# Hybrid recurrent decoder step: sample parts with input buffers and state loads of their own, filler matmuls one contraction step at a time between their state products, and the next mixer's first chunk prepared inside the first of them

## The reference

```
proj = rmsnorm(x) @ w_in                       # 1024 -> 12 x 512 mixer columns, 16 row values, 3 x 1024 gates
A: mLSTM, B: gated DeltaNet, C: HGRN2          # each with a state (heads=4, 128, 128) per sequence
x += w_out( sum_b sigmoid(gate_b) * w_branch_b(mixer_b) )
x += w_down( relu(w_up rmsnorm(x))^2 )
```

```
o_t = S_t^T q_t          S_new = decay * S + sum_s k_s v_s^T      # for each of 8 sequences and 4 heads
```

## Time and profile before

| | |
|---|---|
| time, median of 3 runs | 2506.95 us (2506.61 to 2510.07) |
| the profiled execution | 2505.12 us, of which the span from first to last instruction is 2503.3 us |
| PE busy | 2322.1 us, 93% of the span |
| DVE, ACT, POOL busy | 939.6, 836.6, 635.9 us |
| share of PE in the chain that ended last | 74% |
| mean granted TensorE clock | 0.956 |

### The profile page before, as it was taken

The page is one execution under the profiler, slowest core; times in us unless marked ns, Lnnn a source line. Parts: engine busy times, 40 slices in busy tenths (PEclk is TensorE's granted clock), DMA queues, the critical chain, the costliest instruction groups (busy, mean ns, idle before and its releaser), DMA issues.

```text
span 2503.3 us, 38224 instructions
## 1 busy us (share of the span) xinstructions
PE 2322.1 (93%) x14767; PEld 2255.5 (90%) x14767; DVE 939.6 (38%) x1388; ACT 836.6 (33%) x1477; POOL 635.9 (25%) x433
## 2 busy tenths in 40 slices
PE   4999699999888999999999989996999999999997
PEld 4999699999868999987999979896999999999996
DVE  5756333333135546414444245625212112212214
ACT  4366222322105555422333123323332332332232
POOL 1222223324025445321111132220222222222121
PEclk9999899999868999988999889998999999999998
DMA  4212424222212232235444255420111011111112
GB/s 156 70 60 95 131 80 115 92 80 85 85 55 91 85 110 80 77 99 157 135 135 135 84 168 183 144 100 34 35 47 58 29 50 54 38 42 54 46 34 86
DMA packets 172547, 218.78 MB, mean 87 GB/s; under 512 B 22156, under 2 KB 126476, under 8 KB 172348
## 3 DMA queue, kind: packets, MB, share of 16 engines
q1 hardware_dynamic: 149388, 178.19, 23.9%
q10 hardware_dynamic: 23088, 39.59, 4.2%
HBM read 160.09 MB, written 57.66 MB: 87 GB/s over the span
## 4 chain that ended last, share of the span: by engine, by line
PE 74%; DVE 10%; issue 7%; DMA 4%; ACT 3%; POOL 2%; SPq 1%; DVEq 0%; ACTq 0%; POOLq 0%
PE D L333 59%; PE M L1471 2%; DVE g_dq L773 2%; PE M L1478 2%; PE M L1481 1%; PE M L678 1%; POOL w_lo L314 1%; DVE m_rd L1614 1%; DVE xn_lo L1788 1%; PE M L1700 1%; PE M L1430 0%; ACT g_sg L708 0%; PE M L1497 0%; DMA g_in<-proj 0%; DVE g_Ss L942 0%
## 5 line engine op out<-in xcount | busy, mean ns | idle before, releaser
L333 PE MATMUL D<-xn_hi,w_hi 128*128 128x352 f32 x2808 | 944.2, 336 | 60.9 <-ACT stage L352 29.7
L333 PE MATMUL D<-xn_hi,w_lo 128*128 128x352 f32 x2808 | 911.6, 325 | 0.0
L333 PE MATMUL D<-xn_lo,w_hi 128*128 128x352 f32 x2808 | 911.4, 325 | 0.0
L333 PEld LDWEIGHTS D<-xn_hi,w_hi 128*128 128x128 f32 x2808 | 536.9, 191 | 78.5 <-ACT stage L352 34.8
L333 PEld LDWEIGHTS D<-xn_lo,w_hi 128*128 128x128 f32 x2808 | 538.1, 192 | 4.7 <-issue 3.8
L333 PEld LDWEIGHTS D<-xn_hi,w_lo 128*128 128x128 f32 x2808 | 535.5, 191 | 0.0
L314 POOL TENSOR_TENSOR w_lo<-w_raw,w_hi 128x1024 fp32r<-128x1024 f32 (+1 forms) x105 | 244.2, 2326 | 729.5 <-ACT w_hi L308 729.4
L333 PE MATMUL D<-y_hi,w_hi 128*128 128x352 f32 x960 | 311.1, 324 | 15.0 <-DVE y_lo L1851 11.1
L314 POOL TENSOR_TENSOR w_lo<-e,w_hi 128x512 fp32r<-128x512 f32 (+1 forms) x96 | 164.3, 1712 | 608.1 <-ACT w_hi L308 608.1
L333 PE MATMUL D<-y_lo,w_hi 128*128 128x352 f32 x960 | 311.4, 324 | 0.0
L333 PE MATMUL D<-y_hi,w_lo 128*128 128x352 f32 x960 | 310.8, 324 | 0.0
(11 more groups left out here) (353 smaller groups left out, 2655.0 us busy)
## 6 DMA issues: line engine op xcount, KB each, us to landing
w_raw<-in_w_proj SPq DMA_DIRECT2D x73, 512.0 KB, 3.6
proj<-stage ACTq DMA_DIRECT2D x61, 528.0 KB, 2.7
e<-in_w_full SPq DMA_DIRECT2D x32, 512.0 KB, 3.5
e<-in_w_half SPq DMA_DIRECT2D x64, 256.0 KB, 2.6
stage<-proj SPq DMA_DIRECT2D x24, 528.0 KB, 3.5
d_bc<-rowd SPq DMA_DIRECT2D x32, 256.0 KB, 6.0
m_in<-proj SPq DMA_DIRECT2D x32, 256.0 KB, 3.8
proj<-u_o SPq DMA_DIRECT2D x12, 528.0 KB, 2.9
```

The source lines that it names most:

```text
L333: last = nc.tensor.matmul(D[b][:, 0:GN], w[t.slot][:, k, :], x[:, k, cols], start=(k == 0 and n == 0), stop=(k == kt - 1 and n == 2))
```

## The change

1. **Buffers of their own.** The sample parts read from `sx_*` (gdn), `gx_h` (hgrn), `mx_h` and `mx_bc` (mlstm). SP loads them, and the 2 MB of states, in the middle of the mixer's loop, between chunks 3 and 4; the loop of SP is cut in two for it. The arenas are laid out anew so that the states (all at the same offset) no longer share memory with what the chunks use.
2. **The last chunk prepares the sample part,** in the places where other chunks prepare the next chunk.
3. **Fillers in one-k pieces.** In the sample parts a group of dense work is cut in 8 pieces (3 matmuls each), and a slot stands after each head of state products and after each head's `kv` (`su`) product. `sample_states` is split into decay, spread, add and kv for one head at a time, and these are placed from the first head's output on.
4. **The first HGRN2 chunk** is prepared inside gdn's sample part: its loads are issued at the start of it, and `hgrn_first` (called as `between(0..2)`) and `hgrn_rest` place the six parts. `clear_hg` moves behind the last two adds.
5. SP issues each mixer's first chunk, the prompt state's store and the remaining weight tiles in a new order, and the DMA scratch size is given as 1024.

```diff
-        def sample_states(kind, eng, steps_of, kv, read, S, decay, vt, vx, kt, banks):
+        def sample_states(op, eng, h, steps_of, kv, read, S, decay, vt, vx, kt, banks):
+            if op == "decay":
+                eng.wait_ge(*pe_.after(f"{read}{h}"))
...
+            if op == "spread":
+                if h >= 2:
+                    eng.wait_ge(*pe_.after(f"{kv}{h - 2}"))
...
+            if op == "kv":
+                eng.wait_ge(*dve_.after(f"vx{h}"))
+                if h >= 2:
+                    eng.wait_ge(*dve_.after(f"s2{h - 2}b"))
...
-        def whole_hgrn_prep(kind, eng, sample, slot):
+        def hgrn_first(kind, eng, at):
+            for part in {"dve": [(0,), (1, 2, 3), ()], "act": [(0,), (1,), (2,)], "pool": [(0,)]}[kind][at]:
+                hgrn_prep(kind, eng, 0, 0, part, False)
+            if kind == "dve" and at == 2:
+                clear_hg(eng)
+
+        def hgrn_rest(kind, eng, slot):
+            for some in {"dve": [(4,), (5,), (), ()], "act": [(3,), (4,), (5,), ()], "pool": [(1,), (), (), ()], "pe": [(), (), (), ()]}[kind]:
                 for part in some:
-                    hgrn_prep(kind, eng, 0, 0, part, sample)
-                if at < 4 and not sample:
-                    slot()
+                    hgrn_prep(kind, eng, 0, 0, part, False)
+                slot()
...
+                    if part == 4 and not follows:
+                        eng.wait_ge(ready, 3)
                     for j in range(L)[:4] if part == 4 else range(L)[4:]:
...
+                if sample:
+                    between(0)
+                    eng.wait_ge(*act_.after("vn"))
+                    states("spread", 0)
+                    states("spread", 1)
+                    states("add", 0)
+                    states("spread", 2)
+                    states("add", 1)
+                    states("spread", 3)
+                else:
...
                 if sample:
-                    sample_states(*states)
-                slot()
+                    between(1)
+                    states("add", 2)
+                    states("add", 3)
+                    between(2)
...
                         for b in range(DEC_BATCH):
                             c = h * N + b * DEC_SEQ
-                            i = eng.matmul(M[0][:, c:c + DEC_SEQ], d_Ss[:, b, h, :], d_pb[:, c:c + DEC_SEQ], start=True, stop=True)
-                    i.then_inc(*pe_.step("ks"))
+                            i = eng.matmul(M[0][:, c:c + DEC_SEQ], d_Ss[:, b, h, :], B.pb[:, c:c + DEC_SEQ], start=True, stop=True)
+                        if h == H - 1:
+                            i.then_inc(*pe_.step("ks"))
+                        slot()
...
-        mixers = (("gd", gdn, LOOP_GD, GD_SLOTS, GD_SLOTS, [3, 2, 2, 2, 2, 4] + [3, 3, 3, 3], 3),
-                  ("hg", hgrn, LOOP_HG, HG_SLOTS, HG_SLOTS, [9, 3, 2, 2, 2, 2, 7], 3),
-                  ("ml", mlstm, LOOP_ML, ML_SLOTS, ML_SLOTS, [3, 3, 3, 3, 2, 4], 2))
+        mixers = (("gd", gdn, LOOP_GD, GD_SLOTS, [2, 3, 3, 3, 3, 3, 3, 3, 3, 3, 3, 3, 3, 3, 4, 4, 4] + [5, 4, 4, 4], 3),
+                  ("hg", hgrn, LOOP_HG, HG_SLOTS, [9, 5, 5, 5, 5, 5, 7, 7, 24], 3),
+                  ("ml", mlstm, LOOP_ML, ML_SLOTS, [5, 5, 4, 4, 4, 4, 4, 5, 5, 8], 2))
...
+            chunk_loads(sp, gdn, LOOP_GD, 0, 3)
+            sp.wait_ge(st_out, 16 * 2)
+            gdn("sp", sp, 0, None, True)
+            chunk_loads(sp, gdn, LOOP_GD, 3, NCH - 1)
+            t = LOOP_GD + 2 * NCH
+            load_w(sp, Tile(t), w_proj[t])
+            load_w(sp, Tile(t + 1), w_proj[t + 1])
             stored_all(sp, ML_TILE)
-            mixer_loads(sp, *mixers[1], lambda: None, lambda: out(of_state(s_S), flat_bh(d_Ss), states_out), out_p_H)
+            hgrn("sp", sp, None, lambda: None, False)
+            all_done((gd_pe, gd_dve), NCH)
+            out_p_S()
```

More of the change, by code:

```diff
@@ L858, in prep @@
                     hgrn_prep(kind, eng, n, 1, part, False)
+                elif not sample:
+                    hgrn_prep(kind, eng, 0, 0, part, True)
             def level(j, rows=slice(0, N)):
@@ L1388, in gdn @@
-                ahead()
-                for _ in range(2 * J - (3 if sample else 6)):
-                    slot()
-                if sample:
-                    sample_states(*states)
+                if sample:
+                    for _ in range(9):
+                        slot()
+                    for h in range(H):
+                        states("decay", h)
+                        slot()
+                    between(0)
+                    for _ in range(GX_SLOTS - 14):
+                        slot()
+                else:
+                    for _ in range(6):
+                        slot()
+                    ahead()
+                    for _ in range(2 * J - 5):
+                        slot()
@@ L1664, in mlstm @@
                 slot()
+                if sample:
+                    for _ in range(3):
+                        slot()
                 eng.wait_ge(*dve_.after("h", n))
```

736 lines of the change are left out of this document (437 added, 299 removed).

## The result

The changed kernel takes 2449.78 us (median of 4 runs, 2447.54 to 2455.14) against 2506.78 us for the kernel before on the same chip. The ratio is 0.9774, with a 95% interval of 0.9758 to 0.9791. So the change is worth 57 us, not the 89 us that were forecast, and the time lies 3.8 us above the range.

The account below looks back on a forecast made before the run. PE was taken as the bound, busy 93% but at about half clock in the sample parts. Savings of 43.5 (gdn), 5.2 (HGRN2's first chunk), 23.8 (hgrn) and 16.7 us (mlstm) sum to 89.2, giving 2418 us, range 2403 to 2446.

Parts of the forecast that it names:

- The wait for the inputs: gdn's sample part: PE's 9.58 us wait for inputs goes, since sx_* is loaded some 200 us earlier.
- the one for the spread: gdn's sample part: the 5.84 us wait for DVE's spread of v goes, lying under the next head's products and pieces.
- the one for the copy behind the gate exps: gdn's sample part: the 9.20 us wait for ACT's copy goes, since the exps' load is issued at the stretch's start.
- The new stall: End of gdn's sample part: PE waits 7 us for ACT's copy behind DVE's chain and the exps, plus 2.7 us half clock.
- I take it that the clock holds: Sample parts: full clock despite state products, since runs without a dense piece stay short; mean over 0.95 in hgrn's and mlstm's.
- the longest run without a dense piece: Sample parts: 2.2 us (at and state products), or 4.0 us where the first kv directly follows the last head.
- the same in one part only: Rival: clock falls in one sample part, or for a third of the mixed work; +22 to +37 us, 2440 to 2455; 10%.
- The row used for holding: Profile before the change: the clock didn't fall in 6.2 us of level products, 58 wider matmuls.
- The row that spoke of these products: Profile before the change: clock fell after 2.5 us of only state products, and was 0.50 for the next 11 us.
- what costs nothing, and its cover: Mixers' loops: loading sample inputs and 2 MB of states between chunks 3 and 4 is covered; at most 8 us each.
- that rival 3%: Rival, three loops: the state loads delay the chunks, up to 24 us, 2442; chance 3%.
- the sums: Sample parts' matmul work at full clock, from unit prices: 61.8 us in gdn, 53.3 in hgrn, 42.1 in mlstm.

Follow-up runs that it names:

- Experiment 3: Changed kernel with, in mLSTM's sample part, half of the dense pieces kept back and issued in the middle of a head's state products: 2459.5 us, ratio 0.9792.
- experiment 12: Changed kernel with sooner HGRN2 state loads, early g_kl clearing, later gdn store, more pieces between heads, narrow work behind the last head broken up: 2440.8 us, ratio 0.9735.
- experiment 6: Changed kernel with DVE's clearing of g_kl moved ahead of the spread of head 0: 2453.0 us, ratio 0.9792.
- experiment 9: Changed kernel with sooner HGRN2 state loads, early g_kl clearing, and gdn's state store behind the loads of HGRN2's first pass: 2443.3 us, ratio 0.9731.

## Why the prediction was wrong where it was

**What held.** The idle times were read rightly. The wait for the inputs, the one for the spread and the one for the copy behind the gate exps are gone from gdn. HGRN2's first chunk came from 42.7 to 37.5 us as forecast, and the merge's wait is 11.39 us for 12. The new stall stands at the forecast place with the forecast chain. Its size was off, 3.8 us for 7. Counted from the part's start, DVE ended `y2` at 51.7 us instead of 47, and the copy was done at 67.3 instead of 65.5, so the chain between them took 15.6 us instead of 18.5: the seven differences cost 4.62 us instead of 6.34 and the product 1.2 instead of 1.87. PE, for its part, arrived at 63.6 us instead of 58. The two errors have one cause in common, the half clock behind the last head (699.4 to 706.2), which is 3.4 of these 5.6 us; the two being late together is why the stall came out smaller, which is luck.

**The failed step** is the sentence "I take it that the clock holds", and what it rested on: the longest run without a dense piece, 2.2 us or 4.0. First, it was misread. In mLSTM the last head, the denominators and the sums of k precede the first `kv` without a slot. Second, and more, the length of such a run isn't what decides. Experiment 3 had only short ones, and the clock was at 0.50 for 34 us of its mLSTM part. One head of 2.2 us was enough to bring the clock down with six pieces on either side (experiment 12, mLSTM) and with eight (the same, HGRN2's third head, where the eight ahead of it are 3.8 us at full clock). In the changed kernel this costs, at half of the time spent at 0.50, some 13.7 us in mLSTM (27.3 us at 0.50), 5.1 in HGRN2 (10.2 us), and 3.4 in gdn behind the last head (6.8 us), together 22 us that the forecast had at nothing. The forecast had this as a rival, "the same in one part only", at 2440 to 2455, with a chance of 10%, and this is where the time came out. The clock's price was that rival's lower end. By itself it would have given some 2440 us, inside the forecast's own range; the time left the range because HGRN2's loop (6.9) and the smaller terms below came on top, so that the rival's range holds it is in part luck. The row used for holding, 6.2 us of level products at 1.00, was evidence about other matmuls, 64 columns wide. The row that spoke of these products showed a fall after 2.5 us, and 2.2 is no safe distance from it.

What brings it down isn't settled. Neither the length of a run nor the number of pieces decides: gdn's first block, with heads of 1.84 us and only three pieces between them, ran at 1.00 in all 12 profiled executions that had it mixed. What its heads lack is the product of 32 rows (0.4 us, `at` in gdn's second block) that stands ahead of every other mixed head; no run takes that apart. Why it falls behind the first head in one execution and behind the third in another, with the same code, isn't settled either. The starts of the parts differ between executions by a few us, and the falls last from 3.4 to 34 us. What the runs show is that chance has a share: with one order of PE the parts spread over 9, 6 and 7 us, and the time of a kernel over 6 to 18 us.

The Trainium skill, TensorE: Matmul & The Clock Gate, section A second HAM failure mode: psum-queue depth-cycling, which was cited against the change, has the clock going back and forth between its two levels, and the rows of experiment 12 agree in that. It names small idles of PE as the cause. The records show none: PE is busy for 3.00 of 3.00 and 2.40 of 2.40 us in them. But the ends of matmuls are modelled in a profile, so idles inside a row of narrow products are not excluded.

**The second failed step** is "what costs nothing, and its cover" for the loops: the transfers "have three chunks' time to land". They themselves have, but what is queued behind them hasn't. It cost 5.7 us in one chunk of HGRN2 (8 were the bound). In the two other loops it cost nothing that can be told: gdn's chunks between the first and the last take 46.87 us before and after, and no chunk of mLSTM grew by more than 0.2. The reason stands in the prediction's own account of the first chunk, where the masks came late: DVE's first instruction for the next chunk stands ahead of the running chunk's masks. I gave that rival 3% because of the DMA share, which is a mean and says nothing of order.

**Smaller terms.** The matmul work itself, counted at full clock (PE's busy time less half of its busy time at 0.50), is 64.0, 54.5 and 43.0 us in the three parts, where the sums have 61.8, 53.3 and 42.1, so it was put 0.9 to 2.2 us too low each time. (In mLSTM's sum the small products stand at 4.4 us, where the unit prices say 4.) The sums also leave out PE's waits at the next mixer's door, 1.14 us behind gdn's part and 1.34 behind HGRN2's:

```profile
1101.25 0.65 PE L1835 MATMUL M<-cst,m_in 128*128 128x128 f32 x4 [1.34 <-ACTq L2249]
```

Not explained are 0.9 us up to the last chunk of gdn, 0.7 in mLSTM's loop and 1.3 behind the merge.

## What to carry to other kernels

Matmuls that load a full 128 x 128 weight for four columns can bring the clock down: here it fell between 2.3 us (mLSTM's first head, changed kernel) and 5.2 us (gdn's first block in a lump) after a row of them began. Filling in between them pays where it covers a wait, but can't be counted on to hold the clock, and pieces mixed in evenly may run at half speed themselves. If they are mixed, large blocks of dense work between small ones of narrow work did best (1.5 us or more in HGRN2). Judge by several executions, since the clock falls at other places in the next one.

A prefetch that is itself covered isn't free. Look at what the same queue issues next, who waits for that, and what is queued on that engine behind the wait. Here 2 MB put ahead of a chunk's 0.8 MB cost 5.7 us, and when a stall was removed, one of these transfers came uncovered and took all of the gain back in experiment 6 and some 2 us of it in experiment 9.

When a chain over three engines ends at one door, reordering one engine's stream moves the wait. Shortening the chain removes it. And of two places to wait, the one ahead of dense work costs least.

## What was not expected of the hardware

The granted clock falls with PE busy all the time in the records, and it is down in the work that follows, not in the head itself: a head of state products at 1.00, followed by 3 us of dense pieces at 0.50, four times in a row (experiment 12). Seven DVE differences of 128x256 took 4.62 us without POOL's beside them and 6.34 with them. The Trainium skill, SBUF — State Buffer, section SBUF: two separate sides, has two such instructions exclude one another, and this agrees with it in direction; the remaining 2 us over the 2.62 of `g_ql` lie beside other work of POOL (`w_lo`, 2.40 us). The meeting was moved rather than removed: POOL's seven stand beside DVE's later steps now, take 8.87 us instead of 5.76, and the seven `g_ql` products, 2.62 us before with nothing beside them, take 5.01:

```profile
714.00 4.62 DVE L787 TENSOR_TENSOR g_dq<-g_b 128x256 f32<-128x256 f32 x7
725.53 5.01 DVE L799 TENSOR_TENSOR g_ql<-g_sl,g_dq 128x256 f32<-128x256 f32 x7
```

```profile
715.94 2.40 POOL L328 TENSOR_TENSOR w_lo<-w_raw,w_hi 128x1024 fp32r<-128x1024 f32 x1 [13.21 <-ACT w_hi L322]
719.87 8.87 POOL L832 TENSOR_TENSOR g_dk<-g_b,g_x 128x256 f32<-128x256 f32 x7
```
